# Two sums at a time between halves of weight units, and angle tables in the first iteration, in a two-block transformer kernel

## The reference, cut to what matters

```python
mod = silu(c) @ w_ada + b_ada                      # 6 * 2048 values: sh1 sc1 gt1 sh2 sc2 gt2
h = rmsnorm(x, g_mix) * (1 + sc1) + sh1
proj = h @ w_in                                    # q_a k_a v_a q_b k_b v_b qi ki wi g_a g_b
y_a = stick_breaking_attention(q_a, k_a, v_a)      # 8 heads of 128: "sb"
y_b = dsa_attention(rope(q_b), rope(k_b), v_b, rope(qi), rope(ki), wi)   # 8 heads: "dsa"
x = x + (1 + gt1) * ((sigmoid(g_a) * (y_a @ w_a) + sigmoid(g_b) * (y_b @ w_b)) @ w_o)
h = rmsnorm(x, g_ffn) * (1 + sc2) + sh2            # sh2, sc2, gt2 are wanted only here
```

## Time and profile before

| | us |
|---|---|
| median of 3 runs | 3096.1 |
| lowest, highest run | 3094.66, 3100.26 |
| the profiled execution | 3101.03 |
| its span, first to last instruction | 3099.4 |
| TensorE matmuls busy in it | 2906.7 (94%) |
| VectorE busy | 2023.6 (65%) |
| ScalarE busy | 1344.0 (43%) |
| granted TensorE clock, mean | 0.974 of full |

### The profile page before, as it was taken

The page is one execution under the profiler, slowest core; times in us unless marked ns, Lnnn a source line. Parts: engine busy times, 40 slices in busy tenths (PEclk is TensorE's granted clock), DMA queues, the critical chain, the costliest instruction groups (busy, mean ns, idle before and its releaser), DMA issues.

```text
span 3099.4 us, 61533 instructions
## 1 busy us (share of the span) xinstructions
PE 2906.7 (94%) x24528; PEld 2762.0 (89%) x24528; DVE 2023.6 (65%) x3163; ACT 1344.0 (43%) x1898; POOL 167.2 (5%) x288
## 2 busy tenths in 40 slices
PE   1799999999999999998999999989999999999997
PEld 0799899999988888888999999878889999998997
DVE  7877897777567666664445656665576666664445
ACT  1265334344355555553434444323454444443443
POOL 0111012222000000000000000021000000000000
PEclk7899999999999999999999999999999999999999
DMA  9977578989545555554544555400335555554552
GB/s 387 321 246 246 164 235 266 308 296 312 201 152 185 189 182 189 189 189 151 189 178 148 177 159 163 150 3 4 136 133 178 180 188 181 184 186 159 183 189 95
DMA packets 407684, 586.92 MB, mean 189 GB/s; under 512 B 20416, under 2 KB 368704, under 8 KB 390016
## 3 DMA queue, kind: packets, MB, share of 16 engines
q1 hardware_dynamic: 384864, 517.28, 50.0%
q0 software_dynamic: 20480, 67.13, 6.1%
q10 hardware_dynamic: 2208, 0.66, 0.1%
HBM read 582.91 MB, written 2.10 MB: 189 GB/s over the span
## 4 chain that ended last, share of the span: by engine, by line
PE 83%; DVE 10%; DMA 3%; issue 2%; ACT 2%; SPq 0%; DVEq 0%; POOL 0%; ACTq 0%; POOLq 0%
PE bank L465 18%; PE bank L467 17%; PE bank L466 17%; PE bank L472 15%; PE bank L473 8%; PE bank L1201 3%; DVE wlo L399 2%; DVE ring L2066 1%; DMA late_ring<-w_ada_turned_dram 1%; ACT whi L388 1%; DMA ring<-w_ada_turned_dram 1%; DVE late_ring L2103 1%; PE bank L761 1%; DMA ring<-w_in_dram 1%; DVE mats L2674 1%
## 5 line engine op out<-in xcount | busy, mean ns | idle before, releaser
L399 DVE TENSOR_TENSOR wlo<-ring,whi 128x1024 fp32r<-128x1024 f32 x908 | 1086.9, 1220 | 507.7 <-ACT whi L388 506.2
L388 ACT ACTIVATE whi<-ring 128x1024 fp32r<-128x1024 f32 x908 | 940.2, 1052 | 870.9 <-PE bank L467 574.7
L465 PE MATMUL bank<-hx,whi 128*128 128x256 f32 (+3 forms) x2720 | 783.0, 288 | 29.4 <-DVE wlo L399 22.4
L467 PE MATMUL bank<-hx,wlo 128*128 128x256 f32 (+3 forms) x2720 | 775.4, 285 | 0.0
L466 PE MATMUL bank<-hx,whi 128*128 128x256 f32 (+3 forms) x2720 | 774.8, 285 | 0.0
L472 PE MATMUL bank<-hx,whi 128*128 128x512 f32 x2112 | 741.1, 394 | 1.6 <-DVE wlo L399 1.1
L473 PE MATMUL bank<-hx,wlo 128*128 128x256 f32 x2112 | 591.7, 280 | 0.0
L465 PE MATMUL bank<-xs,whi 128*128 128x256 f32 (+1 forms) x1920 | 543.8, 283 | 23.8 <-DVE xs L458 23.0
L465 PEld LDWEIGHTS bank<-hx,whi 128*128 128x128 f32 x2720 | 517.5, 190 | 42.6 <-DVE wlo L399 19.3
L467 PE MATMUL bank<-xs,wlo 128*128 128x256 f32 (+1 forms) x1920 | 544.2, 283 | 0.0
L466 PE MATMUL bank<-xs,whi 128*128 128x256 f32 (+1 forms) x1920 | 543.9, 283 | 0.0
(11 more groups left out here) (326 smaller groups left out, 2567.9 us busy)
## 6 DMA issues: line engine op xcount, KB each, us to landing
ring<-w_in_dram SPq DMA_DIRECT2D x136, 1024.0 KB, 5.5
ring<-w_up_dram SPq DMA_DIRECT2D x88, 1024.0 KB, 5.1
ring<-w_down_dram SPq DMA_DIRECT2D x88, 1024.0 KB, 4.8
ring<-w_gate_up_dram SPq DMA_DIRECT2D x88, 1024.0 KB, 5.1
late_ring<-w_ada_turned_dram POOLq DMA_DIRECT2D x256, 256.0 KB, 4.5
ring<-w_oab_dram SPq DMA_DIRECT2D x32, 1024.0 KB, 5.5
ring<-w_ada_turned_dram SPq DMA_DIRECT2D x28, 1024.0 KB, 7.6
ring<-w_out_dram SPq DMA_DIRECT2D x16, 1024.0 KB, 5.2
```

The source lines that it names most:

```text
L388: nc.scalar.activation(half_of(whi, u, h, n), ring[:, u % PLAN[phase][3], h * n // 2:(h + 1) * n // 2], ACT.Copy)\
L399: nc.vector.tensor_tensor(half_of(wlo, u, h, n), ring[:, u % PLAN[phase][3], h * n // 2:(h + 1) * n // 2], half_of(whi, u, h, n).bitcast(F ...
L465: nc.tensor.matmul(out_ap, a[0], b[0], start=start, stop=False, **kw)
L467: return nc.tensor.matmul(out_ap, a[1], b[0], start=False, stop=stop, **kw)
```

## The change: sums in pairs, tables moved

Three things. In an iteration of `sb` and of `dsa`, the sixteen late sums stand in eight pairs instead of four groups of four, and `rest_unit` is taken apart so that a pair stands between the two halves of units 2 (sb, dsa), 3, 4 and 5. The angle tables 0 and 1, made ahead of `sb` before, are made inside its first iteration. The four sines stand together at the end of ScalarE's first iteration. No instruction is added or removed. The diff is whole:

```diff
--- before.py
+++ after.py
@@ -1599,9 +1599,6 @@
                 round_unit("sb", 3, i)
                 if not first(i):
                     sb_softplus(i)
-                else:
-                    sine(0)
-                    sine(1)
                 round_unit("sb", 4, i)
                 round_unit("sb", 5, i)
                 if not first(i):
@@ -1611,8 +1608,8 @@
                     attended(i, o_done, yaT)
                     step.end()
                 else:
-                    sine(2)
-                    sine(3)
+                    for n in range(4):
+                        sine(n)
             rotated(act, 4, sb)
             step.leave(3)
 
@@ -2091,8 +2088,6 @@
             dve.wait_ge(consts_in, 16)
             phase_end(dve, 1, meet=False)
             phase_end(dve, 2, meet=False)
-            turn(0)
-            turn(1)
             dve.wait_ge(c_ready, 3)
 
             def late_sum(b, j, c, cs, at):
@@ -2137,29 +2132,41 @@
                 dve.wait_ge(d_done, i * 2)
 
             def sb(i, last):
-                rest_unit("sb", 2, i)
-                rest_unit("sb", 3, i)
+                rest_half("sb", 2, i, 0)
+                late(0, i, 0, 2)
+                rest_half("sb", 2, i, 1)
+                rest_half("sb", 3, i, 0)
+                late(0, i, 2, 4)
+                rest_half("sb", 3, i, 1)
                 if not first(i):
                     sb_masked(i)
                 multiplied(dve, "sb", 1, i)
                 nc.vector.tensor_copy(qT[:].rearrange("p a t -> p (a t)"), bank[:, 0, :]).then_inc(q_read, 1)
-                late(0, i, 0, 4)
-                rest_unit("sb", 4, i)
+                rest_half("sb", 4, i, 0)
+                if first(i):
+                    turn(0)
+                late(0, i, 4, 6)
+                rest_half("sb", 4, i, 1)
                 if not first(i):
                     sb_softplus(i)
-                late(0, i, 4, 8)
-                rest_unit("sb", 5, i)
+                late(0, i, 6, 8)
+                rest_half("sb", 5, i, 0)
+                late(0, i, 8, 10)
+                rest_half("sb", 5, i, 1)
+                if first(i):
+                    turn(1)
                 multiplied(dve, "sb", 3, i)
                 nc.vector.tensor_copy(kT[:].rearrange("p a t -> p (a t)"), bank[:, 1, :]).then_inc(k_read, 1)
                 if not first(i):
                     sb_differences(i)
-                late(0, i, 8, 12)
+                late(0, i, 10, 12)
                 ahead(rest_unit, "sb", i, last)
+                late(0, i, 12, 14)
                 multiplied(dve, "sb", 5, i)
                 if not first(i):
                     dve.wait_ge(o_done, i * 2)
                 nc.vector.tensor_copy(vS[:].rearrange("p a t -> p (a t)"), bank[:, 2, :]).then_inc(v_read, 1)
-                late(0, i, 12, KD)
+                late(0, i, 14, KD)
                 if first(i):
                     turn(2)
                     turn(3)
@@ -2283,24 +2290,32 @@
 
             def dsa(i, last):
                 step.begin(i - 1, 10)
-                rest_unit("dsa", 2, i)
-                late(1, i, 0, 4)
-                rest_unit("dsa", 3, i)
+                rest_half("dsa", 2, i, 0)
+                late(1, i, 0, 2)
+                rest_half("dsa", 2, i, 1)
+                rest_half("dsa", 3, i, 0)
+                late(1, i, 2, 4)
+                rest_half("dsa", 3, i, 1)
                 dsa_masked(i)
                 multiplied(dve, "dsa", 1, i)
                 rope(qT[:].rearrange("p a t -> p (a t)"), bank[:, 0, :], 2 * T, tabs128, 64, q2_read, i + 1)
-                rest_unit("dsa", 4, i)
+                rest_half("dsa", 4, i, 0)
+                late(1, i, 4, 6)
+                rest_half("dsa", 4, i, 1)
                 dsa_probs(i)
-                late(1, i, 4, 8)
-                rest_unit("dsa", 5, i)
+                late(1, i, 6, 8)
+                rest_half("dsa", 5, i, 0)
+                late(1, i, 8, 10)
+                rest_half("dsa", 5, i, 1)
                 multiplied(dve, "dsa", 3, i)
                 rope(kT[:].rearrange("p a t -> p (a t)"), bank[:, 1, :], 2 * T, tabs128, 64, k2_read, i + 1)
-                late(1, i, 8, 12)
+                late(1, i, 10, 12)
                 ahead(rest_unit, "dsa", i, last)
+                late(1, i, 12, 14)
                 multiplied(dve, "dsa", 5, i)
                 dve.wait_ge(o2_done, i * 2)
                 nc.vector.tensor_copy(vS[:].rearrange("p a t -> p (a t)"), bank[:, 2, :]).then_inc(v2_read, 1)
-                late(1, i, 12, KD)
+                late(1, i, 14, KD)
                 step.end()
             with dve.Fori(1, 3) as i:
                 dsa(i, False)
```

## The result

The changed kernel takes 3108.1 us (median of 9 runs, 3102.9 to 3110.4) against 3096.6 us before (9 runs, 3094.7 to 3100.7): +11.5 us by the medians, a ratio of 1.0032 with a 95% interval of 1.0024 to 1.0041, that is +7 to +13 us. The forecast was +12.0 us, 3108.1.

What follows compares the result with a forecast made beforehand. TensorE, busy 94% of the span, was taken as the bound, so only its waits and clock falls move the end. The terms summed to +12.0 us on 3096.1, forecast 3108.1 us, range 3098 to 3117.

Steps and rivals of the forecast that it cites:

- Iteration 0, +1.0: First iteration of sb: moving the tables leaves VectorE idle 5.0 us for a late tile; +1.0 us, bounds 0 and +3.0.
- rival (d): Late tiles collide with ring loads, and waits between two halves of one unit stop TensorE: 3114 us and more; chance 0.12.
- Iteration 1, +3.7: In sb, pairs ahead of masks (2.4) and softplus sums (1.2) delay TensorE: +3.7 us, stop 1.95 becomes 5.6.
- Iterations 2 and 3, +1.2 each: In sb, the pair ahead of the softplus sums costs 1.2 us each time; sums 0 to 3 nothing, up to +1.
- The clock, +5.1: Half clock behind three longer TensorE stops in sb, 1.7 us each: +5.1 us, bounds 0 and 6.8.
- dsa: Its iterations 1, 2 and 3: +1.2, +0.5 and -1.9 us (iteration 3 at best -3.7, at worst 0); no clock fall counted.
- (b): Faster: late tiles arrive in time everywhere, with ScalarE, not VectorE, last before the softplus sums; -7.8 us, 3088 us; chance 0.06.
- (a): Only the waits grow and the clock holds: +6.9 us, 3103 us; chance 0.18.
- (c): No change: whole dsa gain (-3.7), at most one clock fall, iteration 0 free; +5.8 to +1, 3100 us; chance 0.14.

Runs made afterwards that it cites:

- e10: The changed kernel once more, unaltered, in one execution: 3107.1 us.
- e6: The changed kernel plus twelve matmuls on constants by TensorE ahead of its wait for the softplus sums in iterations 1 to 3 of sb: 3102.5 us.
- e8: The changed kernel with sums 4 to 7 of sb all between the halves of unit 4, ahead of the softplus sums: 3112.3 us.
- e4: The changed kernel with sums 4 and 5 of sb behind the softplus sums, not between the halves of unit 4: 3104.5 us.
- e1: The kernel before with only angle tables 0 and 1 moved inside sb's first iteration and the four sines together, late sums in fours: ratio 1.0000.
- e2: The changed kernel with tables and sines put back and dsa as before, leaving only the pairs in sb: 3108.1 us.
- e5: The changed kernel with sums 0 to 3 of sb put back behind the masks and the query copy: 3100.8 us.
- e3: The kernel before with only the pairs in dsa, sb and tables unchanged: 3097.0 us, ratio 1.0003.
- e9: The kernel before with only iteration 0 of sb reordered: table 0 behind unit 2's first half, the other tables later, sums in pairs: 3093.4 us against 3095.1.
- e7: The changed kernel with e9's iteration 0 and later sums moved behind masks (sb), softplus and probabilities: 3088.6 us, ratio to before 0.9975.

## Why the prediction was right, point by point

**Iteration 0, +1.0.** Right in this profile and in e10: A +1.05 and +1.12 us, with a wait of 4.83 us for the first tile (5.0 predicted) and a stop of 1.23 us at 144. With the same text A was +2.3 us in e6, inside the bound of +3.0. In e8 and e4 the sums 4 to 7 stand otherwise in iteration 0 too; A was +1.2 and +4.5 there, the latter with the wait of 3.15 us that rival (d) had foreseen. And the cause is the two edits together: e1 alone -0.6, e2 alone +0.1.

**Iteration 1, +3.7.** B +3.67 us. Its parts are 2.44 (e5 takes it away) and 1.23 (e4 takes it away), and e8 adds another 1.23: the length of the sums queued ahead, to 0.02 us in seven profiles. The stop of 5.6 us came out as 4.59 because TensorE was itself 1.0 us later, from a half clock that lasted longer in front of it (0.64 over 7 us against 0.80); in e10 with 0.76 it read 5.43. The distance, not the stop, was what the sum needed.

**Iterations 2 and 3, +1.2 each.** Too small. Without a clock fall (e6) C is 2.0 and D 1.7 us over before: 1.2 for the pair and 0.8 and 0.5 for the pair 0, 1, whose tile came late and held the last half of unit 3. That was the stated upper part of the term (up to +1), worked out as fitting by 0.5 us; the 3.21 us wait shows that it did not. e5 takes both remainders away, and e4, which lacks the pair 4, 5, still has D +0.6 against before.

**The clock, +5.1.** The mechanism is shown (e6). The price was 1.5 to 1.6 and not 1.7 us where the window reads 0.76 or 0.77 (e3 1.64, e6 1.53 and 1.54, e9 1.49), and more where half clock lasted longer: C, laid beside that of e6, is 2.3 us more in e2 (0.70) and 2.4 in e10 (0.58). One price for every fall was too simple. In this profile two of the three falls came: behind 4.59 and 3.16 us, not behind 2.92. This and the term before it missed in opposite directions: 2.4 + 5.1 = 7.5 predicted, 3.56 + 3.22 = 6.8 measured in C and D.

**dsa.** Iteration 1 +1.22 in every kernel with the pair there (F), and a fall behind the 2.45 us stop, which was not counted. Iterations 2 and 3: no stop in either; G is 2.2 us shorter in spite of that fall, so the gain was near the best case of -3.7 and not the -1.9 taken; iteration 2 cost nothing. Of F and G, +1.22 is the pair, +1.4 the fall (from L976 to the next L976: 39.21 us, 37.78 before) and -3.6 iteration 3 and what follows. Together -1.0 us at the first L465 of `merge`, where the terms said -0.2.

**Sum and rest.** At the end of `sb` +11.5 us (12.2 predicted), with `dsa` +10.5, where the terms say 12.0 and the medians +11.5. That the forecast meets the median to 0.1 us is luck: the interval is +7 to +13 us, several terms missed in opposite directions, and two of three falls came in one execution and another two of three in the next. The mechanism, term by term, is what was right. That the two profiled spans differ by 2.7 only was not in the change: between the 2.71 us stop in the `qi` stage and the start of `dsa`'s unit 2, a stretch with no edit in it, the changed kernel took 46.6 us and the one before 49.3, because the clock fell behind that stop in one and not in the other (0.56 over 7 us from 351.2 against 1.00). The changed kernel's window:

```profile
362.00:369.00 7.00, 6.68 (x55) 6.21 (x56) 6.83 (x13) 3.64 (x6) 0.00 (x0) 1.00 0.48 150
```

In all twelve profiles this stretch is 46.6 to 46.8 us (e1, e4, e6, e8, e9 and the changed kernel), 49.3 to 49.5 us (before, e2, e5, e7, e10) or 47.9 (e3). At the first L465 of `merge` the changed kernel is still 7.6 us behind the one before. It makes up another 4.7 us after that, in stages that the change does not touch; where they come from is not shown.

Of the rivals, (b) wanted ScalarE, not VectorE, last in front of the softplus sums; e4 and e8 show that VectorE's order is. (a) is out, since the clock fell and e6 shows that the falls cost. Of (c) only the gain in `dsa` came. What stays open: why the late tiles fall otherwise in e6 than in the two profiles of the changed kernel, when the clock falls behind a stop, and which of the edits in e7 beyond iteration 0 gives how much; its G and its last stretch before the fourth L879 group (27.1 us, 28.5 before) were not taken apart.

## What to carry to other kernels

Spreading filler work evenly is not the aim: put it where its engine would idle, and never between the input and the instruction that another engine is standing for. In this kernel a pair put ahead of the masks or of the softplus sums cost its own length, 1.22 us; the same pairs behind them cost nothing that B, C and D of e7 show. Before moving work out of a place, look what will wait there instead (here a tile that had not landed), and compare kernels by distances between fixed instructions, since both the stop lengths and single spans move with the clock.

## What the runs showed of the hardware that was not expected

**A stop's cost depends on more than its length.** Behind stops of 1.95 us (before), 2.92 us (changed) and 3.09 us (e10) the clock stayed full, behind 1.96, 2.27 (e7, 0.76 over the next 7 us) and 2.45 us it fell to half for some 3.4 us. In e3 the clock fell behind the first L879 stop of the unchanged stage, where it had not fallen before. The Trainium skill (TensorE: Matmul & The Clock Gate, "What's actually happening") says that the monitor's window runs free of the kernel, and these profiles agree in so far as the same place of the same text fell in one execution and not in the other (the second L879 stop, 3.16 and 3.09 us). Between those two the stretch in the `qi` stage differs by 2.7 us.

**Late tiles land late beside a ring load.** In the 4 us of the earlier trace rows the queue of the ring moved 1.28 MB and the late tiles' queue nothing, though four late tiles were asked for in that time and took 6.5 us to land (median). In the 6 us before, the late queue moved 1.05 MB and the ring's 0.41, and three tiles took 3.6 us. The Trainium skill (DMA: Bandwidth & Descriptors, "Queues, rings and completion order") says that each DMA engine takes turns between the queues it has work for, packet by packet. The row does not look like turns; but from 138 to 139 us of the changed kernel both moved, 0.22 MB of late tiles and 0.13 MB of the ring. Whether the late queue had its descriptors ready in the stretch of the row no run here shows.
